# Turning three expert blocks in the gap of the first layer norm of an attention, gating and expert block, on one core

## What is computed

```python
proj = x @ w_in                                  # q, k, v, su, sv, two gates
y_na = neighbourhood_attention(q, k, v, na_rpb)
y_sg = spatial_gating(gelu(su), gelu(sv), ...)
merged = sigmoid(ga) * (y_na @ w_branch_na) + sigmoid(gb) * (y_sg @ w_branch_sg)
x = layer_norm(DN_ALPHA * x + merged @ w_out, ln1_g, ln1_b)      # the first layer norm
# expert layer: 8 heads, 128 + 128 keys, the best 16 of 16384 experts per head and token
q = x @ wq
ids, g = product_key_top16(q, subkeys1, subkeys2)
a = einsum('td,thkd->thk', x, u_tab[ids])
y = einsum('thk,thkd->td', gelu(a) * g, v_tab[ids])
x = layer_norm(DN_ALPHA * x + y, ln2_g, ln2_b)
```

## Time and profile before

| what | value |
|---|---|
| median of three runs | 1057.58 us (1056.67 to 1060.58) |
| the profiled execution: its time, its span | 1056.79 us, 1055.0 us |
| busy: PE, PE weight loads | 1032.4 us (98%), 927.3 us (88%) |
| busy: DVE, ACT, POOL | 843.2 us (80%), 456.9 us (43%), 449.9 us (43%) |
| granted TensorE clock, mean | 0.996 of full |
| DMA, mean over the span | 211 GB/s |

### The profile page before, as it was taken

One profiled execution on the slowest core, in us unless ns is written; L12 is line 12 of the kernel. 1 busy time (PEld: TensorE's weight loads), 2 busy tenths in 40 slices (PEclk: granted clock), 3 DMA queues, 4 the chain that ended last, 5 costly groups with the idle time before them and its releaser, 6 DMA issues.

```text
span 1055.0 us, 20427 instructions
## 1 busy us (share of the span) xinstructions
PE 1032.4 (98%) x6763; PEld 927.3 (88%) x6763; DVE 843.2 (80%) x1541; ACT 456.9 (43%) x658; POOL 449.9 (43%) x332
## 2 busy tenths in 40 slices
PE   8989999999999999999999999998999999999996
PEld 8878898899999999999999999834888888888885
DVE  3476457887999999888888888514999999999887
ACT  4374434544434434444444444202444454444442
POOL 3910000048888888788888888872000000000000
PEclk9999999999999999999999999999999999999998
DMA  9875679645666565977777777699888888988772
GB/s 319 245 276 205 231 263 310 221 130 101 140 140 140 140 139 140 202 169 168 167 176 173 163 173 165 139 317 301 273 270 263 270 270 267 267 275 265 244 242 97
DMA packets 153955, 223.06 MB, mean 211 GB/s; under 512 B 48448, under 2 KB 99456, under 8 KB 153920
## 3 DMA queue, kind: packets, MB, share of 16 engines
q1 hardware_dynamic: 116480, 221.17, 65.8%
q0 software_dynamic: 37440, 1.43, 9.9%
HBM read 204.59 MB, written 17.96 MB: 211 GB/s over the span
## 4 chain that ended last, share of the span: by engine, by line
PE 46%; POOL 38%; issue 8%; DVE 3%; DMA 2%; ACT 1%; SPq 0%; POOLq 0%; DVEq 0%; ACTq 0%
POOL expert_weights L507 38%; PE ps L1447 29%; PE ps L1350 14%; DMA expert_weights<-gw,cell 1%; PE ps L1239 1%; ACT w_hi L630 1%; DVE w_lo L980 1%; PE ps L1217 1%; DMA xres<-in_x_dram 0%; DVE small L751 0%; PE ps L1183 0%; PE ps L1227 0%; DMA v_raw<-in_peer_v_dram 0%; DVE v_lo L1083 0%; DVE xres L1139 0%
## 5 line engine op out<-in xcount | busy, mean ns | idle before, releaser
L507 POOL DMA_INDIRECT expert_weights<-gw,cell x256 | 412.0, 1609 | 249.9 <-DVE gw L967 165.6
L1391 PE MATMUL ps<-act_hi,uT_hi 128*128 128x256 f32 x1024 | 295.7, 289 | 0.0
L1391 PE MATMUL ps<-act_hi,uT_lo 128*128 128x256 f32 x1024 | 290.5, 284 | 0.0
L1391 PE MATMUL ps<-act_lo,uT_hi 128*128 128x256 f32 x1024 | 290.2, 283 | 0.0
L716 ACT ACTIVATE v_hi<-v_raw 128x512 fp32r<-128x512 f32 x256 | 147.8, 625 | 208.7 <-PE ps L1447 161.0
L1391 PEld LDWEIGHTS ps<-act_hi,uT_hi 128*128 128x128 f32 x1024 | 197.0, 192 | 0.0
L1391 PEld LDWEIGHTS ps<-act_lo,uT_hi 128*128 128x128 f32 x1024 | 197.0, 192 | 0.0
L1391 PEld LDWEIGHTS ps<-act_hi,uT_lo 128*128 128x128 f32 x1024 | 196.7, 192 | 0.0
L1083 DVE TENSOR_TENSOR v_lo<-v_raw,v_hi 128x512 fp32r<-128x512 f32 x256 | 165.0, 686 | 13.7 <-ACT v_hi L716 11.7
L1447 PE MATMUL ps<-v_hi,hid_hi 128*128 128x512 f32 x464 | 144.9, 392 | 4.3 <-DVE hid_lo L1100 4.2
L1447 PE MATMUL ps<-v_lo,hid_hi 128*128 128x512 f32 x464 | 144.2, 391 | 0.0
(11 more groups left out here) (167 smaller groups left out, 1441.5 us busy)
## 6 DMA issues: line engine op xcount, KB each, us to landing
v_raw<-in_peer_v_dram SPq DMA_DIRECT2D x152, 512.0 KB, 4.4
u_raw<-in_peer_u_dram SPq DMA_DIRECT2D x68, 512.0 KB
u_raw<-in_peer_u_dram SPq DMA_DIRECT2D x240, 128.0 KB
w_raw<-in_w_in_dram SPq DMA_DIRECT2D x8, 2048.0 KB, 9.0
expert_weights<-zeros SPq DMA_DIRECT2D x16, 1024.0 KB, 11.8
g_in<-expert_weights SPq DMA_DIRECT2D x104, 128.0 KB, 3.4
w_raw<-in_peer_wq_dram SPq DMA_DIRECT2D x4, 2048.0 KB, 10.7
w_raw<-in_w_out_dram SPq DMA_DIRECT2D x2, 2048.0 KB, 9.2
```

The lines of the kernel that those rows point to most:

```text
L507: pool.indirect_dma_start(out=table_cells, out_offset=bass.IndirectOffsetOnAxis(ap=cell[:, t, k:k + 1], axis=0), in_=gw[:, t, k:k + 1], in ...
L1391: ins = pe.matmul(ps[:, bank, 0:T], (uT_hi, uT_hi, uT_lo)[part][:, slot, k, :], (act_hi, act_lo, act_hi)[part][:, k, :], start=(k == 0 and ...
```

## The change

TensorE's 30 turns of the identity become 10, and ahead of them stand the transposes of expert blocks 0 and 1, which go into the two accumulators while these are free. The transposes of block 2 stand behind those of the normed rows. ScalarE copies blocks 0 and 2 from PSUM to the SBUF tile `uT_raw`, VectorE copies block 1; the accumulators are needed again by `w0` and `w1`, which wait for the copies. Later, at the places where the blocks were rounded from PSUM before, they are rounded from `uT_raw`. The loads of the blocks move in SP's order: blocks 0 and 1 behind the load of `w0` and its two parts of zeros, block 2 behind the load of `w1` and its part of zeros, and behind a wait for the transposes of block 0.

```diff
-NORMING = 30
+NORMING = 10
+SAVED = 3
...
@@ SP, in the loop over chunks, behind the chunk's load and its zeros
+            if n_chunk == "w0":
+                sp.wait_ge(s["mrg_lo_done"], 2)
+                for n in range(2):
+                    load_u(block_of(n), n)
+            if n_chunk == "w1":
+                sp.wait_ge(s["u_read"], 1)
+                load_u(block_of(2), 0)
...
-        sp.wait_ge(s["mrg_lo_done"], 2)
-        for n in range(2):
-            load_u(block_of(n), n)
-        for n in range(2, NPRE):
+        for n in range(SAVED, NPRE):
@@ ScalarE
+        def save_turned(n, j):
+
+            act.wait_ge(s["u_read"], n + 1)
+            act.activation(uT_raw[:, n].rearrange("p a b -> p (a b)"), acc(j), ACT.Copy).then_inc(s[f"saved{n}"], 1)
+
+        def round_saved(n):
+
+            act.wait_ge(s[f"saved{n}"], 1)
+            act.activation(uT_hi[:, n].rearrange("p a b -> p (a b)"), uT_raw[:, n].rearrange("p a b -> p (a b)"),
+                           ACT.Copy).then_inc(s["uT_hi_done"], 1)
...
+            if hc == HC["w0"] + 1:
+                save_turned(2, JOB["w1"])
             if hc == HC["w0"]:
+                save_turned(0, JOB["w0"])
                 sqrt_var(1, TB)
@@ VectorE
                 dve.tensor_scalar(xres[:, 0, :], xres[:, 0, :], mv[:, 0:1], rstd[:, 0:1], ALU.subtract,
                                   ALU.mult).then_inc(s["first_normed"], 1)
+                dve.wait_ge(s["u_read"], 2)
+                dve.tensor_copy(uT_raw[:, 1].rearrange("p a b -> p (a b)"), acc(JOB["w1"])).then_inc(s["saved1"], 1)
@@ TensorE
             if hc == NHC - 1:
 
-                pe.wait_ge(s["act_lo_done"], 8)
-                transpose_u(16, 0, 6)
                 pe.wait_ge(s[f"acc_free{JOB['w2'] % 2}"], JOB["w2"] // 2 + 1)
-                transpose_u(16, 1, 2)
...
+                if name in ("w0", "w1") and first:
+                    pe.wait_ge(s["saved0" if name == "w0" else "saved2"], 1)
...
                     keep_busy(NORMING)
+                for n in range(2):
+                    j = JOB[f"w{n}"]
+                    pe.wait_ge(s[f"acc_free{j % 2}"], j // 2)
+                    transpose_u(16, n, 2 * (j % 2))
                 transpose_rows([(s["first_normed"], 1), (s["second_normed"], 1)], free_banks)
+                pe.wait_ge(s["saved1"], 1)
+                transpose_u(32, 0, 2 * (JOB["w1"] % 2))
...
-                if not (last and k == 3):
+                if not (last and k == 3) and not (head and k + 2 < SAVED):
```

More of the change, by code:

```diff
@@ L255, in hybrid_block @@
              "g_fill_in0", "g_fill_in1", "g_fill_in2", "g_fill_in3", "fill_hid", "fill_done",
-             "u_in0", "u_in1", "u_in2", "u_in3", "v_in0", "v_in1", "v_in2", "v_in3", "u_read", "u_turned", "uT_hi_done", "uT_lo_done", "v_hi_done",
+             "u_in0", "u_in1", "u_in2", "u_in3", "v_in0", "v_in1", "v_in2", "v_in3", "u_read", "saved0", "saved1", "saved2", "u_turned", "uT_hi_done", "uT_lo_done", "v_hi_done",
              "v_lo_done", "a_done", "act_done", "hid_done", "hid_m", "hid_h", "y_first", "y_half", "y_done", "out_ready",
@@ L310, in zero_part, with load_u @@
             sp.dma_start(part, zeros[:].unsqueeze(1).broadcast_to([P, per, ZEROS])).then_inc(s["zeroed"], 16)
+        def load_u(b, slot):
+            sp.dma_start(u_raw[:, slot, :], u_dram[bass.ds(b * P, P), :]).then_inc(s[f"u_in{slot}"], 16)
         for c, n in enumerate(CHUNKS):
@@ L334, in _ @@
                 sp.dma_start(sgn_b[:], sg_norm_b[0:1, :].broadcast_to([P, W5])).then_inc(s["sgn_in"], 16)
+            n_chunk = n
             for n in range(ZERO_AT.get(c, 0)):
                 zero_part(sum(ZERO_AT.get(before, 0) for before in range(c)) + n)
+            if n_chunk == "w0":
[5 more added lines that the diff above has]
+                load_u(block_of(2), 0)
             if c == 5:
@@ L341, in _ @@
                 sp.dma_start(ln1bT, ln1_b[0].rearrange("(p k) -> p k", k=KD)).then_inc(s["ln1T_in"], 16)
-        def load_u(b, slot):
-            sp.dma_start(u_raw[:, slot, :], u_dram[bass.ds(b * P, P), :]).then_inc(s[f"u_in{slot}"], 16)
         def load_u_squares(b, slot):
@@ L661, in _ @@
                 for n in range(2):
-                    round_uT(n, 6 - 4 * n, uT_hi[:, n])
+                    round_saved(n)
+            if hc == HC["w0"] + 1:
+                save_turned(2, JOB["w1"])
             if hc == HC["w0"]:
+                save_turned(0, JOB["w0"])
                 sqrt_var(1, TB)
@@ L690, in _ @@
             if n + 2 <= NPRE:
-                round_uT(n + 2, 6 - 4 * (n % 2), uT_hi[:, (n + 2) % 4])
+                if n + 2 < SAVED:
+                    round_saved(n + 2)
+                else:
+                    round_uT(n + 2, 6 - 4 * (n % 2), uT_hi[:, (n + 2) % 4])
                 for batch, after in enumerate(EXP_AFTER, EARLY):
@@ L898, in pick, with rest_saved @@
                 top16(cv[:, t, h, :], cpos[:, t, h, :], c, cand2[:])
+        def rest_saved(n):
+            dve.wait_ge(s["uT_hi_done"], n + 1)
+            dve.tensor_tensor(uT_lo[:, n].rearrange("p a b -> p (a b)"), uT_raw[:, n].rearrange("p a b -> p (a b)"),
+                              uT_hi[:, n].rearrange("p a b -> p (a b)").bitcast(F32), ALU.subtract) \
+                .then_inc(s["uT_lo_done"], 1)
         def rest_uT(n, banks, slot):
@@ L910, in pre_split @@
             for n in range(2 + splits_by(before), 2 + splits_by(before + cost)):
-                rest_uT(n, 6 - 4 * (n % 2), n % 4)
+                if n < SAVED:
+                    rest_saved(n)
+                else:
+                    rest_uT(n, 6 - 4 * (n % 2), n % 4)
             return before + cost
@@ L1026, in _ @@
                 for n in range(2):
-                    rest_uT(n, 6 - 4 * n, n)
+                    rest_saved(n)
             if HC["w0"] < hc <= HC["w0"] + TB:
```

## The result

The changed kernel takes 1061.05 us in the median (1058.66 to 1063.85, 20 runs) beside 1057.68 us of the kernel before (20 runs): a ratio of 1.003, 95% interval 1.0021 to 1.0039, or 3.3 us more. It is slower, as forecast, but by 0.3% and not by 0.8%: inside what was called no change (up to 0.5%), and inside the stated range of 1058.5 to 1069.0 us.

What follows compares the result with a forecast made beforehand. PE bounds up to 214 us, then POOL's scatters to 724.05 us, then PE. Block 2 landing at 200.7 us, 0.9 us of transposes and 1.7 us of clock delay w0 and the end by 8.5 us: 1066.1 us, range 1058.5 to 1069.0.

Steps and rivals of the forecast that it cites:

- What bounds: PE's dense part bounds up to 214 us, POOL's 256 scatters from 223.64 to 724.05 us, then PE to the end.
- So the side of PE is about 3.8 us ahead of POOL when they meet: Near 724 us SP and PE wait about 3.8 us for the last scatter, with the filled part's work all issued.
- What PE saves between 224 and 724 us is worth nothing.: The 2.7 us of transposes taken from PE behind the first scatter only lengthen its slack: 0 us.
- Blocks 0 and 1 in the gap: Between o1 and w0, PE turns both blocks by 190.35 us, ahead of the normed rows at 190.92: 0 us.
- ScalarE's copy: Copying block 0 ahead of the table load and square root, between o1 and w0, delays the square root by 1.35 us.
- Block 2: Its load queues behind w1 and zeros and lands at 200.7 us; PE stands 6.3 us ahead of w0.
- The clock: Behind PE's wait for block 2 the granted clock falls to about 0.52 for 3.5 us, costing 1.7 us.
- The sum: w0, the first scatter and the end come 8.5 us later; median 1066.1 us.
- the meeting: At about 724 us, where PE's side waits for POOL's last scatter; PE's saving was to give nothing back there.
- rival A: Block 2's load does not queue and lands at 193.0 us; only the square root's 1.35 us remain: 1058.9 us; 12%.
- The signs of being wrong: Wrong if block 2 is turned before 197 us, or the first scatter and the end do not move by the same amount.
- B: Faster or not slower: PE's 2.7 us come through at 724 us, where its side is last; 1056.2 or 1054.9 us; 5%.

Runs made afterwards that it cites:

- after: Profiled execution of the changed kernel, unaltered; span 1062.0 us, own time 1063.85 us, the highest of its 20 runs.
- e1: The changed kernel once more, unaltered, for a second profile (span 1059.1 us); ratio 1.0042 to the kernel before.
- e9: The kernel before, with only the first of 8 transpose pieces made for blocks 0 to 2; ratio 0.9989 to the kernel before.
- e5: e3 with ScalarE's copy of block 0 moved behind the second normalisation; ratio 0.998 to the kernel before.
- e12: The version of e5 once more on another draw of runs; ratio 0.9982 to the kernel before.
- e2: The changed kernel with only blocks 0 and 1 turned in the gap, block 2 where it was before; ratio 1.0006 to the kernel before.
- e3: The changed kernel with block 2 loaded early, with blocks 0 and 1, into its own place of u_raw; ratio 0.9998 to the kernel before.
- e7: The changed kernel with the 1 MB of zeros behind w1's load moved behind w2's load; ratio 0.9994 to the kernel before.
- e10: The changed kernel with 2 MB of zeros instead of 1 behind w1's load, ahead of block 2; ratio 1.0073 to the kernel before.
- before: The kernel without the change; first profile span 1055.0 us, median 1057.68 us beside the changed kernel.

## Why the prediction was wrong, point by point

- **What bounds.** Right up to 214 us and for the scatters: the piece from `w0` to the first scatter is 28.89 to 28.91 us in every profile with a full clock there, and the scatters take 494.5 to 496.4 us whatever is ahead of them.
- **"So the side of PE is about 3.8 us ahead of POOL when they meet", and "What PE saves between 224 and 724 us is worth nothing."** The first holds, the second failed. The wait's length was right, but the waiting side's loads delay the very landing that it waits for. A saving of 1.8 to 2.7 us (the prediction's 0.9 us for each of two or three blocks) moves them out of its way: last scatter to PE takes 7.4 to 8.4 us instead of 9.7 to 10.2. SP's wait for the last scatter was to grow to 6.5 us and grew only to 4.5 (after) and 5.3 (e1). Since the scatters vary by up to 1.8 us and the part behind PE's start by up to 2.2 us, a single profile shows less at the end than at this place; the timed gain is 1.1 us in e9 (not clear of nothing) and 2.0 in e5 and e12, where other engines' work had moved as well.
- **Blocks 0 and 1 in the gap: 0 us.** Right. In after there was no wait for them, in e1 one of 0.23 us.
- **ScalarE's copy: "1.35 us later for everything behind it".** Right in mechanism and size: 1.37 us in after, e1, e2 and e3, and gone in e5, where the copy stands behind.
- **Block 2: "the landing is at 195.9 + 4.5 to 5.0 = 200.4 to 200.9 us".** The mechanism was right (in the order of the queue, e7 and e10) and the term was 3 us too large. PE was to start on block 2 at 13.3 us behind the end of `o1` and did so at 10.3 (after) and 10.2 (e1). The step that failed is the charge for the bytes of blocks 0 and 1: that 1.05 MB more ahead of `w1` and the zeros costs its full time, 3.0 to 3.4 us at 346 to 312 GB/s, on top of the old landing at 195.9 us. But the zeros landed 8.9 us behind the end of `o1` (183.21 + 14.0 - 188.30) beside 8.5 before (182.32 + 13.6 - 187.41): 0.4 us for both blocks. `w1` landed 12.0 us behind its issue, beside 11.7. Block 2 itself landed 1.2 us behind the zeros, where 1.5 to 1.7 us had been counted. The two landings in after:

```profile
w_raw<-in_peer_wq_dram SPq DMA_DIRECT2D x1, 2048.0 KB, 12.0
...
expert_weights<-zeros SPq DMA_DIRECT2D x1, 1024.0 KB, 14.0
```

A share of 1.01 at 346 and 0.98 at 312 GB/s had been read as full engines; with more in the queue the same stretch moved 391 GB/s, and from 184 to 188 us 409 instead of 251. Taking a better rate for the added 1.57 MB alone would not have saved the forecast: at 409 GB/s it is 3.8 us, and block 2 comes at 12.3 us. The bytes that were there before moved faster too. Why, no run here shows.

- **The clock: "I take the 1.7 us".** In the two profiles either nothing (e1) or 2.4 us: 0.7 us in the transposes and first matmuls up to `w0` and 30.61 - 28.89 = 1.7 us behind. Over the runs, (1 - mean granted clock) times span is 7.3 us for after and 7.1 us for e1, and 5.6, 6.6, 5.9 and 6.2 us for the four sets of runs of before: 0.5 to 1.7 us more on average, and 1.5 us for e1 beside its own set. The size was about right for the mean, by luck. Behind the longer wait of e10, 6.06 us, it was 1.2 us (0.7 up to `w0` and 0.5 behind): there the clock fell (0.82 from 196 to 198 us) while PE still waited, until 201.33 us.
- **The sum.** Measured parts: 3.7 us (square root, wait and transposes of block 2, no low clock), about 1.6 us clock, about 1.8 us back at the meeting: 3.5 us, beside the 3.3 us timed. The parts are not known better than to a microsecond: the scatters took 0.9 us and the last part 0.5 us more in after and e1 than in the two profiles of before, and whether that is more than chance is open. Forecast: 8.5 us = 3.7 + 3.1 (bytes ahead of block 2) + 1.7 + 0. The range held the measured time only because it had been widened for rival A.
- **The signs of being wrong.** They did not work. Block 2 was turned at 198.56 us in after and at 196.97 us in e1, on both sides of the 197 us named. The first scatter and the end moved by 7.1 and 7.0 us in after, as if nothing had come back; 3.1 and 4.1 us in e1. One pair of profiles cannot show a give-back of 1.8 us at the end of a run; the pieces between named events can.
- **The rivals.** A (block 2 does not queue) is wrong, though its time, 1058.9 us, was nearer to the measured 1061.05 than the forecast's 1066.1: luck. B had the right idea, that PE's saving comes through, but not the place: it needs no change of which side is last.

## What to carry to other kernels

A DMA issued late, into a queue that already holds megabytes, must not be what the engine on the chain waits for next: the same work was free when its load was issued with the others into a place of its own. A busy share of 1 does not say that the engines are at their rate (here 312 GB/s, and 391 GB/s with more in the queue), so bytes added ahead of a transfer can cost anything from nearly nothing (0.4 us for 1 MB of blocks 0 and 1) to their full time (2.1 and 2.8 us for 1 MB of zeros); forecast with both ends. And a side that waits can still be worth speeding up, if its transfers stand beside those that it waits for.

When work is put into a wait, look at what stood in that wait on every engine: here a table load of 1.28 us, which the new copy pushed out of it and onto the path.

## What the runs showed of the hardware that was not expected

- The DMA engines' busy share was 0.98 at 312 GB/s and 1.03 at 391 GB/s in the same stretch of two kernels that differ by 1 to 1.5 MB of loads.
- Behind waits of 3.24 and 3.32 us of TensorE the granted clock once stayed at full (e1) and once fell to 0.52 for 7 us (after). In e2 it fell behind waits of only 1.61 and 1.79 us around the transposes of the normed rows; with waits of 1.61 and 0.92 us (e3) or 1.61 and 1.15 us (e7) there it stayed. In before it was low behind 3.75 us at 724 us. It can also fall inside a wait: 0.81 from 196 to 198 us in after, where PE did nothing.
- The last indirect scatter landed (by SP's next issue) 5.7 and 6.4 us behind its issue where a 512 KB load was issued 1.3 to 1.5 us behind it, 4.0 to 5.1 us where the last such load was issued 0.3 to 1.1 us ahead of it, and 4.4 us where it came only behind the landing.
